# Order of exponentials, rotations and copies in a transformer block, and constant matmuls in TensorE's pauses

## The reference, cut to what matters

```python
# first block
u = rms_norm(h, pre_mix_gain[l])                     # 16 meta tokens + 256 tokens
proj = u @ w_in[l]
qa, ka, va, qb, kb, vb, g = jnp.split(proj, SPLITS, axis=-1)
qa = rope(qa...); ka = rope(ka...)                   # rotary embedding of Q and K
qb = rope(qb...); kb = rope(kb...)
o_swa = windowed_gqa_sink_attention(qa, ka, va, attn_sink[l], pos, is_real)
o_diff = differential_attention(qb, kb, vb, lam, lambda_init, diff_subln_gain[l], is_key)
merged = g_swa * (o_swa @ w_branch_swa[l]) + g_diff * (o_diff @ w_branch_diff[l])
...
# second block: gated delta rule in chunks of 64, beside a sparse attention
a_mat = jnp.where(strict, beta[..., :, None] * kk * decay, 0.0) + jnp.eye(CHUNK)
sol = lax.linalg.triangular_solve(a_mat, rhs, left_side=True, lower=True, unit_diagonal=True)
```

## Time and profile before

| | |
|---|---|
| time, median of 3 runs | 1019.86 us |
| lowest and highest | 1014.61 and 1020.11 us |
| the profiled execution, its own time | 1020.14 us |
| its span, first to last instruction | 1018.3 us |
| granted clock of TensorE, mean | 0.991 |
| PE busy | 976.7 us, 96% |
| DVE busy | 685.3 us, 67% |
| ACT busy | 536.3 us, 53% |
| weights and other reads | 150.76 MB |

### The profile page before, as it was taken

How to read it: one execution, slowest core, us unless ns; L and a number is a source line. 1 busy time by engine, 2 the same in 40 slices (tenths; PEclk the granted TensorE clock), 3 DMA queues, 4 the chain that set the end, 5 groups by cost and what they waited for, 6 DMA issues and landing times.

```text
span 1018.3 us, 16659 instructions
## 1 busy us (share of the span) xinstructions
PE 976.7 (96%) x6754; PEld 888.3 (87%) x6754; DVE 685.3 (67%) x1264; ACT 536.3 (53%) x1039; POOL 109.8 (11%) x137
## 2 busy tenths in 40 slices
PE   6999999999999999999999999899899999999997
PEld 5888999888999988888889998888799998888886
DVE  5766665666666777676658578975765467767674
ACT  6666566565445653444446685553444354434443
POOL 1111100010100200000001118901100000000001
PEclk9999999999999999999999999999999999999999
DMA  9433242333544755656565563210343255455541
GB/s 321 128 124 125 84 163 86 125 125 111 180 166 129 254 174 193 208 179 209 167 207 184 180 212 95 72 42 1 125 161 129 83 187 207 165 207 168 204 166 41
DMA packets 126107, 154.97 MB, mean 152 GB/s; under 512 B 2728, under 2 KB 117680, under 8 KB 125648
## 3 DMA queue, kind: packets, MB, share of 16 engines
q1 hardware_dynamic: 123616, 142.91, 42.2%
q0 software_dynamic: 1952, 10.61, 3.0%
q10 hardware_dynamic: 464, 0.40, 0.2%
HBM read 150.76 MB, written 3.16 MB: 151 GB/s over the span
## 4 chain that ended last, share of the span: by engine, by line
PE 70%; DVE 13%; ACT 11%; issue 2%; DMA 1%; POOL 1%; POOLq 0%; DVEq 0%; SPq 0%; ACTq 0%
PE ps L778 13%; PE ps L779 7%; PE ps L1062 5%; PE ps L754 5%; PE ps L756 4%; PE ps L755 4%; ACT whi L1954 4%; PE ps L1035 4%; PE ps L1036 4%; DVE wlo L1301 3%; PE ps L1037 3%; PE ps L798 3%; PE ps L800 3%; PE ps L799 3%; PE ps L745 3%; ACT SC L1954 3%
## 5 line engine op out<-in xcount | busy, mean ns | idle before, releaser
L1301 DVE TENSOR_TENSOR wlo<-raw,whi 128x1024 fp32r<-128x1024 f32 x268 | 324.9, 1229 | 227.2 <-ACT whi L1954 226.3
L1954 ACT ACTIVATE whi<-raw 128x1024 fp32r<-128x1024 f32 x268 | 274.3, 1050 | 142.6 <-PE ps L779 53.8
L778 PE MATMUL ps<-R1b,whi 128*128 128x512 f32 x576 | 201.8, 393 | 0.0
L754 PE MATMUL ps<-R1b,whi 128*128 128x256 f32 (+1 forms) x592 | 174.8, 295 | 0.4 <-ACT SC L1954 0.4
L756 PE MATMUL ps<-R1b,wlo 128*128 128x256 f32 (+1 forms) x592 | 168.8, 285 | 0.0
L755 PE MATMUL ps<-R1b,whi 128*128 128x256 f32 (+1 forms) x592 | 168.5, 285 | 0.0
L779 PE MATMUL ps<-R1b,wlo 128*128 128x256 f32 x576 | 161.4, 280 | 0.0
L778 PEld LDWEIGHTS ps<-R1b,whi 128*128 128x128 f32 x576 | 108.1, 188 | 24.7 <-issue 0.5
L754 PEld LDWEIGHTS ps<-R1b,whi 128*128 128x128 f32 x592 | 112.9, 191 | 11.1 <-issue 8.1
L755 PEld LDWEIGHTS ps<-R1b,whi 128*128 128x128 f32 x592 | 112.7, 190 | 0.4 <-issue 0.2
L756 PEld LDWEIGHTS ps<-R1b,wlo 128*128 128x128 f32 x592 | 112.9, 191 | 0.0
(11 more groups left out here) (295 smaller groups left out, 2035.3 us busy)
## 6 DMA issues: line engine op xcount, KB each, us to landing
raw<-in_w_in SPq DMA_DIRECT2D x35, 1024.0 KB, 5.1
raw<-in_w_ffn_in SPq DMA_DIRECT2D x22, 1024.0 KB, 5.1
raw<-in_w_ffn_out SPq DMA_DIRECT2D x11, 1024.0 KB, 5.4
raw<-in_w_gate SPq DMA_DIRECT2D x11, 1024.0 KB, 5.1
raw<-in_w_up SPq DMA_DIRECT2D x11, 1024.0 KB, 5.3
raw<-in_w_down SPq DMA_DIRECT2D x11, 1024.0 KB, 5.7
raw<-in_w_out SPq DMA_DIRECT2D x8, 1024.0 KB, 5.2
raw<-in_w_xkv SPq DMA_DIRECT2D x8, 1024.0 KB, 5.7
```

The costliest lines, as they stand in the source:

```text
L754: e.matmul(o, hi[:, kt, c], R[0][:, kt, 0:n], start=kt == 0, stop=False)
L778: e.matmul(B[:, :].rearrange("p (a n) -> p a n", a=2), hi[:, kt, c], R[2][:, :, kt, 0:256], start=kt == 0, stop=False)
L1301: e.tensor_tensor(half_of(wlo[i % HL], i, k), half_of(raw[i % RAW], i, k), f32(half_of(whi[i % HL], i, k)), SUB).then_inc(lo_split(i, (i, k)))
L1954: return e.activation(o, i, f, **kw)
```

## The change

`x0` and `x1` get side 0. `spread` puts them in a list, `behind_split`, and the next `take` appends them behind the splits that it appends itself, ahead of its own half. The rotation on DVE and POOL becomes a step of its own, `rotate`, behind the next yield of the generator, which is behind the parts that stand on side 1 of that half, the maxima `s0` and `s1` among them; ACT's copies stay in `rope`. `swap` and `setup` move behind the first half of the first V. And a new helper of TensorE, `keep`, multiplies constants into a bank whose content nobody reads: 13 times with 256 columns ahead of everything, 6 times with 128 columns ahead of `ssq` of K and of `wide`, and 20 times ahead of level 1 of `lev_a`.

```diff
-STAGES = {"swa": ((0, 1, "s0"), (1, -1, "x0"), (1, 1, "s1"), (2, -1, "x1"), (3, 1, "p0"), (4, 1, "p1"), (5, 1, "v"),
+STAGES = {"swa": ((0, 1, "s0"), (1, 0, "x0"), (1, 1, "s1"), (2, 0, "x1"), (3, 1, "p0"), (4, 1, "p1"), (5, 1, "v"),
...
     def take(i, j):
         ahead(taken=1)
+        while behind_split:
+            step(*behind_split.pop(0))
         halves.append((i, j))
...
                 if (at, side) == (k, -1):
                     step(*token)
+                if (at, side) == (k, 0):
+                    behind_split.append(token)
...
             step("rope", key, 2 * u + j, j, i, state["rope"])
             state["rope"] += 1
             yield 1
-        if key == "ka0":
-            step("swap")
-            step("setup")
+            step("rotate", key, 2 * u + j, state["rope"] - 1)
...
-    units = [opening(), rope("ka0", 1024, 0), values("va", 1280, 0), qa[1], ga[0], qa[2], ...
+    va = behind(values("va", 1280, 0), ("swap",), ("setup",))
+    units = [opening(), rope("ka0", 1024, 0), va, qa[1], ga[0], qa[2], ...
...
+            def keep(B, n, a=ident, b=ident):
+
+                for _ in range(n):
+                    e.matmul(B[:, 0:b.shape[1]], a, b, start=True, stop=True)
...
                 if name == "ssq":
                     B = claim("small", ("ssq", k), (delta_dve, ("ssq", k)))
+                    keep(B, 6 if k else 0)
...
                 if name == "wide":
-                    p.wait_ge(delta_pool, "rn")
                     for t in range(2):
                         B = claim("small", ("wide", t), (delta_dve, ("kt", t)))
+                        if t == 0:
+                            keep(B, 6)
+                            p.wait_ge(delta_pool, "rn")
...
                 if name == "lev_a":
                     for t in range(2):
                         B = claim("small", ("t1", k, t), (delta_act, ("t1", k, t)))
+                        keep(B, 20 if (k, t) == (1, 0) else 0)
                         p.wait_ge(delta_dve, ("ls", k, t))
...
+            p.wait_ge(set_dve, "half")
+            keep(banks[7].t, 13, half[:, 0:1].to_broadcast([128, 128]), half[:, 0:1].to_broadcast([128, 256]))
             for now[0], (name, *a) in enumerate(plan):
```

More of the change, by code:

```diff
@@ L163, in skew @@
         yield 1
[L167 removed]
+STAGES = {"swa": ((0, 1, "s0"), (1, 0, "x0"), (1, 1, "s1"), (2, 0, "x1"), (3, 1, "p0"), (4, 1, "p1"), (5, 1, "v"),
                   (6, 1, "t")),
[L169 removed]
+          "diff": ((0, 1, "s0"), (1, 0, "x0"), (1, 1, "s1"), (2, 0, "x1"), (3, -1, "c"), (4, 1, "p"), (5, 1, "v"),
                    (7, -1, "n"), (8, 1, "t"))}
@@ L213, in schedule @@
 def schedule():
-    plan, order, halves, done = [], [], [], set()
+    plan, order, halves, done, behind_split = [], [], [], set(), []
     state = {"rope": 0}
@@ L312, in opening @@
             if j:
-                step("roped", "qa", 0, 0)
-                step("roped", "qa", 1, 1)
+                for b in range(2):
+                    step("roped", "qa", b, b)
+                    step("rotate", "qa", b, b)
                 state["rope"] = 2
@@ L1415, in swa @@
                             par("sink", 2 * g + h), ADD, MAX, mx[:, u:u + 1]).then_inc(head_dve(("max", x, u)))
-                if part in ("x0", "x1"):
-                    t = int(part[1])
                     c = slice(2 * t, 2 * t + 2)
@@ L1942, in vector @@
             e.memset(ones, 1.0).then_inc(set_dve("one"))
-            parts = {"split": split, "rows": rows, "turn": turn, "turnx": turnx, "stat": stat_, "rsb": rsb_, "chunk": chunk, "chunk2": chunk2, "upg": upg, "setup": setup, "rope": rope, "roped": roped, "turnm": turnm, "vt": vt, "swa": swa, "diff": diff,
+            parts = {"split": split, "rows": rows, "turn": turn, "turnx": turnx, "stat": stat_, "rsb": rsb_, "chunk": chunk, "chunk2": chunk2, "upg": upg, "setup": setup, "rotate": rotate, "turnm": turnm, "vt": vt, "swa": swa, "diff": diff,
                      "bsw": bsw, "bdf": bdf, "merge": merge, "post": post, "upu": upu, "zc": zc, "tail": tail, "taps": taps, "zg": zg,
@@ L2489, in gpsimd @@
             pool.wait_ge(set_dve, "half")
-            parts = {"rows": rows, "roped": roped, "rope": rope, "swa": swa, "diff": diff, "between": between, "post": post, "cbload": cbload, "smallload": smallload,
+            parts = {"rows": rows, "rotate": rotate, "swa": swa, "diff": diff, "between": between, "post": post, "cbload": cbload, "smallload": smallload,
                      "kvout": kvout, "kvin": kvin, "taps": taps, "delta": delta, "dsa": dsa, "dsah": dsah, "stat": stat_, "g3load": g3load, "final": final}
```

11 lines of the change are left out of this document (3 added, 8 removed).

## The result

The changed kernel takes 1003.98 us (median of 4 runs, 1002.43 to 1005.27), the kernel before 1019.73 us (median of 4, three of them those of the first table): the ratio of the means is 0.9856, with an interval from 0.9822 to 0.9891. The forecast was 1009.5 us with a range down to 1005.5. The profiled execution took 1004.01 us, and its span is 1002.2 us against 1018.3.

What follows compares the result with a forecast made beforehand. PE bound the kernel, busy 976.7 of 1018.3 us. Terms 2.0 + 2.3 + 0.36 + 5.3 + 0 + 0.5 = 10.5 us from 1020.14 gave 1009.7, at the median 1009.5 us, range 1005.5 to 1015.5.

Steps and rivals of the forecast that it cites:

- The heads and V: First block's heads and first V: PE waits removed, 2.3 us at V, 0.36 at 24.89 us, 5.3 in the heads.
- The 5.3 us: Heads: exponentials behind the split remove 80% of 6.6 us of PE waits (3.5 on DVE, 3.1 on ACT).
- No wait of PE on a rotated tile is in the trace. Price nothing by itself; it is part of the 80%: Heads, rotations moved behind the maxima: maxima come earlier, the rotation later, no gain of its own.
- The exponential is no later where the split has its inputs when ACT gets there: Heads, ACT: its split, about 1.05 us, falls into its average 2.5 us wait, so moving exponentials behind it adds nothing.
- Start: Constants ahead of everything: second unit begins at 19.3 us, not 21.35, worth 2.0 us; bounds 3 loss to 4.2 gain.
- Low stretches: Low-clock stretches at 307.9 and 676.6 us cost 2.9 us; fewer pauses should leave fewer, worth 0.5 us.
- no low stretch any more: Rival, chance 0.09: the 2.9 us of the two low-clock stretches and all the waits are gained, 1005.7 us.
- Delta stage: Constants there: low stretches at 615.1 and 645.8 hidden, gain 0; overrun hidden, cost 0; bounds 2.8 gain, 1.5 loss.
- Every sign: Early 28 matmuls in 3 us; second unit about 19.3; no V wait; ACT's `swa` waits down a third; PE's under 2.5.
- The heads' waits stay: Rival, chance 0.17: PE's waits in the heads stay, behind matmuls and copies that keep their order; 1015.2 us.
- a start that doesn't pay: Rival, chance 0.12: clock stays low on constants or drops during transposes; 1014.4 us at worst, 1011.4 if gain is lost.
- Slower: Rival, chance 0.05: an ACT split waiting for PE or its load holds exponentials; 1032 us at 0.7 us a pair.

Runs made afterwards that it cites:

- e14: The kernel before, unchanged, profiled once more: 1017.22 us in one execution.
- e7: The changed kernel without the 13 products of constants at the start: 1006.45 us.
- e10: The changed kernel with 4 products of constants at the start in place of 13: 1006.61 us in one execution.
- e15: The changed kernel without the constants at the start, the same kernel as e7, once more: 1006.24 us in one execution.
- e9: The kernel before with exponentials behind the next split and DVE's negations left in the exponentials' step, so behind the split too: 1020.24 us, ratio 1.0016.
- e2: The kernel before with only the rotations moved behind the maxima, as a step of their own: 1010.63 us, ratio 0.9922.
- e13: The changed kernel with the negations back in the exponentials' step, so behind DVE's part of the split: 1014.33 us, ratio 0.9952.
- e1: The kernel before with only exponentials moved behind the next split on ACT and DVE's negations right behind the maxima: 1009.82 us, ratio 0.9919.
- e6: The changed kernel with the exponentials and the negations put back ahead of the splits: 1006.49 us.
- e4: The kernel before with only the 13 products of constants at the start added: 1017.41 us, ratio 0.9981.
- e8: The changed kernel without the constants in the delta stage: 1004.44 us.
- e3: The kernel before with only swap and setup moved behind the first half of the first V: 1016.11 us, ratio 0.9981.
- e11: The changed kernel with 12 constants ahead of the output projection's first unit and 64 columns in place of one in the sums of squares: 1003.16 us, ratio 0.9847.

## Why the prediction was right in direction and short in size

Of the 5.6 us between the 10.5 forecast and the 16.1 of the profiled executions, about 4.5 lie in the heads and at V, 1.0 in a low stretch and 0.4 in the delta stage; 0.1 goes off at the start. (The sum is 10.46, so it gives 1009.4 us; the 1009.5 comes of rounding.)

**The heads and V: the term that was mis-sized.** The prediction took 2.3 + 0.36 + 5.3 = 8.0 us; the part measures 12.4. Three things make up the difference in size.

First, "I take 80%" of 6.6 us. All of the waits went: 1.3 us.

Second, the idle time that a row shows was taken for the whole price of a wait. Two stretches of the timeline of PE in the kernel before:

```profile
33.91 0.29 PE L756 MATMUL ps<-R1b,wlo 128*128 128x272 f32 x1
36.49 0.55 PE L745 MATMUL ps<-ca,SD 128*128 128x128 f32 x3 [2.29 <-ACT SD L1954]
...
50.82 0.73 PE L899 MATMUL ps<-F 64*128 64x272 f32 x4
...
55.06 1.44 PE L899 MATMUL ps<-F 64*128 64x272 f32 x4
```

From the start at 33.91 to the next at 36.49 are 2.58 us, and such matmuls otherwise start 0.125 us apart: 2.46 us were lost, where the idle column has 2.29, since the matmul's drawn end lies some 0.17 us behind the moment at which the next could start. Over the nine pauses that is 10.7 us in place of 9.3: another 1.4 us.

Third, waits inside rows that group several matmuls are no pauses in any list. The second pair of rows is the same group of four score products, 0.73 us long and then 1.44. Of 32 such groups two are long, 0.9 us together. PE's 2141 matmuls of this part are the same in the same order in both kernels, so their starts can be compared one by one: 10.9 us of the 12.4 arise at the nine pauses, 0.9 in the two long groups, 0.2 in a short pause at 70.7 us and 0.4 in two groups of products with V. That leaves 0.1. One of the nine, at 24.89 us, goes with an early start and not with the swap: in e14, the kernel before once more with its second unit at 19.30 us, it is gone and the heads take 284.76 us, 0.6 less. In e7, e10 and e15 it is there and the heads take 273.5, 0.5 more than in the changed kernel. The prediction's reason for it, that PE's first unit ends earlier, was right.

**Whose gain it is: the step that failed.** The 5.3 us were derived from DVE's idleness in the lock step of the earlier trace rows, and given to the exponentials. That is not what the pauses hang on: e9 takes this idleness away (26.8 us of 82.0 left) and gains nothing, e2 leaves 75.4 of it and gains 9.1 us. What counts is when the negated maximum comes out. The step "No wait of PE on a rotated tile is in the trace. Price nothing by itself; it is part of the 80%" was wrong. e2 gains 9.1 us in the heads with rotations alone. The trace did not hide it: the rotation stood on DVE between ACT's copies and the maxima, and the maxima let out the negation, for which ACT stood 80.8 us. I looked only at who waits for the rotation's result, not at what stood behind it in DVE's list. At the earlier trace rows it held the first maximum back to 49.32 us, where e2 has it at 47.89. And the exponentials were priced without their negations. "The exponential is no later where the split has its inputs when ACT gets there" is true only where the negation stays ahead of DVE's part of the split; e9 and e13 show what it costs otherwise, 2.3 and 9.4 us. That either link takes about 9 us (e1, e2) and that the exponentials with their negations add only 1.1 us to the rotations (e6 against the changed kernel) is measured. The reverse, the changed kernel without its rotations, was not run; e1's 276.56 us less 2.5 at V and 0.5 at 25 us would be 273.6, so an estimate from these for what the rotations add is 0.7 us. That it is one ring of copies, rotation, maxima, negation, exponential, split and the next copies is read from the order and the waits.

**Start: 2.0 forecast, 1.86 measured**, with DVE's `wlo` as the wait that sets the end, as argued. With the pause at 24.89 us an early start is worth some 2.4 us. But what the constants remove is a chance and not a fixed cost, as the last section shows: e14 had the early start without them. The medians of e4 and of the kernel before beside it lie 0.8 us apart.

**Low stretches: 0.5 forecast, 1.5 measured.** The one behind the merge wait is missing in the profiled execution of the changed kernel, and the last one stayed. That is luck as far as these runs show: 8 of the 17 profiled executions had one there, three of them in kernels that are the changed one less one edit (e6, e7, e8). The rival "no low stretch any more" had the prices right (2.9 us for two; 1.5 each measured). Its 1005.7 us was still too long, for it took the same too short pauses in the heads.

**Delta stage: 0 forecast, 0.36 in the profile.** Right, for the reason given, and e14 has 0.31 of the 0.36 without constants. The low stretches at 615 and 646 us were hidden by waits: with both present e4 took 145.95 us, with neither e6 took 145.78.

**The signs and the rivals.** Every sign that was to show the forecast right came, but none of them tells rotations from exponentials. "The heads' waits stay" did not come, nor did a start that doesn't pay. "Slower" did not come. e13 shows that late exponentials do hold the scores' banks, and that this costs some 10 us, but it is the negation behind DVE's part of the split that makes them late there. The rival's own cause, a split of ACT that waits for PE and holds the exponentials, made no pause of PE in the changed kernel.

## What to carry to other kernels

When two engines wait for each other in turn, list the whole ring with what stands ahead of each link in each engine's list; breaking one link can give nearly all of the gain, breaking the next adds little, and moving one half of a pair (a consumer without its producer) can cost more than leaving both. That an engine stands idle between two others' work is no price: ask whether anything late hangs on it. Price a wait from start to start of the instructions around it less their usual spacing, and compare lengths of like groups, since the idle column leaves out part of a wait. Where low-clock stretches move between executions, compare parts of the timeline cut at the same instructions, not single times.

## What the runs showed of the hardware that was not expected

**The rise of the clock at the start is up to the execution.** With 13 constants ahead, the second unit began between 19.42 and 19.59 us in all six profiled kernels that have them. Without them, or with four, it began at 19.30, 19.49 and 19.84 us in three executions and at 21.14 to 21.97 in eight, with one kernel on both sides twice (before and e14; e7 and e15).

**Transposes can raise the clock.** In e14 24 transposes were all that PE had done, and the products behind them ran at the high pace, 0.12 us a matmul from 13.26 us; so it was in e3 and e7. The row of 23 shows it too: it takes 4.42 us at the low level (before) and 2.45 at the high one (changed kernel), but 3.73 in e14 and 4.01 in e3, where the starts go from 0.21 us apart to 0.11 at about 12 us (e14). In the eight late executions the same transposes did not do it, and the clock rose some 4 us into the products. The Trainium skill, "TensorE: Matmul & The Clock Gate", Part 4, says that transposes do not count as busy for the clock, beside a measurement in bf16, and the prediction had the trace agree. These runs, with float32, disagree, and the one row on which that agreement stood was one of the late executions. PEclk showed 1.00 from 14 to 17 us in the late execution of the earlier trace rows and in the early one of e14 alike. It shows 1.00 wherever it stands ahead of the trace's first clock entry, which is the first rise (17.8 us before, 12.1 in e14); in e10, which has an earlier one, it shows 0.50. The spacing of the matmuls tells the pace.

**The kernel before has three times.** Of the 15 runs beside e9 to e11 one took 1015.2 us, six 1017.5 to 1018.1 and eight 1020.0 to 1020.6, and the 19 beside e1 fall into the same three groups, on another chip. Two of its executions were profiled, 1020.14 and 1017.22 us (e14): of the 2.9 us between them 2.05 are the start, 0.59 the pause at 24.89 us that goes with it, and 0.31 lie between 590 and 737 us. Low stretches make such a step as well: e4, whose profiled execution started early, has runs at 1014.3 us with a mean clock of 0.995 and at 1017.5 with 0.991. Which of the two makes which step of the kernel before in the other runs was not settled.

**A low stretch needs more than a pause.** Pauses of 1.0 to 2.7 us and of 0.6 us near the end of the delta stage stand in every profiled kernel. Behind them a low stretch ran in 13 of the 17 profiled executions, and none in e4, e6, e9 and e11. The first three have none of e11's edits. Whether e11's edits, 64 columns in place of 1 or the 12 constants, keep it away is open; all five of its executions had a mean clock of 0.999.
